# State space scan with head sums spread by one selector product, input stage merged with setup, narrow products by features, attention logits on both halves of the rows

## What is computed

```python
def mamba2_mixer(u, w_in, conv_w, conv_b, dt_bias, a_log, d_skip, norm_w, w_out):
    zxbcdt = u @ w_in                       # 1024 -> z 2048, xbc 4096, dt 32
    xbc = silu(causal_depthwise_conv(xbc, conv_w, conv_b))
    dt = softplus(dt_raw + dt_bias);  a = -exp(a_log)
    y = ssd_chunked_scan(xh * dt, dt * a, bm, cm)      # 32 heads in 8 groups
    ...
def stick_breaking_attention(u, w_q, k, v, w_o):       # 16 heads of 64
    z = einsum("bhqd,bhkd->bhqk", qi, kj)              # logits
    ...
```

## Time and profile before

| what | value |
|---|---|
| runs | 2638.74, 2640.85, 2643.32 us, median 2640.85 |
| profiled execution | 2641.31 us, span 2639.5 us |
| TensorE busy | 94% of the span |
| VectorE / ScalarE / GpSimd busy | 38% / 22% / 57% |
| mean granted TensorE clock | 0.964 of full |

### The profile page before, as it was taken

The page is one execution under the profiler, slowest core; times in us unless marked ns, Lnnn a source line. Parts: engine busy times, 40 slices in busy tenths (PEclk is TensorE's granted clock), DMA queues, the critical chain, the costliest instruction groups (busy, mean ns, idle before and its releaser), DMA issues.

```text
span 2639.5 us, 34935 instructions
## 1 busy us (share of the span) xinstructions
PE 2490.9 (94%) x14538; PEld 2019.2 (77%) x14538; DVE 1003.8 (38%) x1619; ACT 571.3 (22%) x1155; POOL 1494.0 (57%) x1396
## 2 busy tenths in 40 slices
PE   8998998999999999999999998998688998999998
PEld 6777886788888888558888887675477687888887
DVE  3443748155033400334512435775632332421023
ACT  1112322012011011760201101345443210110010
POOL 7554556568587486335867746471121664666663
PEclk9997999999999999999999998999798999999999
DMA  5222022223233233002332322130000232333321
GB/s 170 72 58 72 1 73 88 88 94 105 82 104 102 61 121 101 8 16 89 104 96 93 99 64 87 45 96 24 1 4 3 92 96 72 104 96 96 96 80 64
DMA packets 104290, 199.07 MB, mean 75 GB/s; under 512 B 9306, under 2 KB 12612, under 8 KB 104132
## 3 DMA queue, kind: packets, MB, share of 16 engines
q1 hardware_dynamic: 101476, 189.36, 23.0%
q10 hardware_dynamic: 2656, 7.47, 0.8%
HBM read 194.71 MB, written 2.10 MB: 75 GB/s over the span
## 4 chain that ended last, share of the span: by engine, by line
PE 84%; DVE 9%; ACT 3%; POOL 2%; issue 2%; SPq 0%; DMA 0%; DVEq 0%; POOLq 0%; ACTq 0%
PE psum L153 35%; PE psum L293 23%; PE psum L155 8%; PE psum L232 3%; PE psum L1253 1%; POOL weight_split_ring L412 1%; PE psum L968 1%; PE psum L1262 1%; PE psum L194 1%; DVE big L873 1%; PE psum L982 1%; PE psum L1281 1%; DVE big L1821 1%; DVE best L1820 1%; POOL weight_split_ring L409 0%
## 5 line engine op out<-in xcount | busy, mean ns | idle before, releaser
L412 POOL TENSOR_TENSOR weight_split_ring<-weight_ring,weight_split_ring 128x512 fp32r<-128x512 f32 (+2 forms) x732 | 953.6, 1323 | 30.6
L153 PE MATMUL psum<-x_split,weight_split_ring 128*128 128x512 f32 x4080 | 958.5, 394 | 1.9 <-POOL weight_split_ring L412 1.3
L153 PEld LDWEIGHTS psum<-x_split,weight_split_ring 128*128 128x128 f32 x4080 | 766.8, 189 | 171.9 <-issue 11.6
L409 POOL TENSOR_SCALAR weight_split_ring<-weight_ring 128x1024 fp32r<-128x1024 f32 (+2 forms) x366 | 395.2, 1080 | 735.2 <-PE psum L293 340.7
L293 PE MATMUL psum<-weight_split_ring,hidden_split 128*128 128x512 f32 x2448 | 576.6, 396 | 8.2 <-DVEq L2931 8.2
L293 PEld LDWEIGHTS psum<-weight_split_ring,hidden_split 128*128 128x128 f32 x2448 | 460.4, 188 | 120.0 <-DVEq L2931 8.6
L155 PE MATMUL psum<-weight_split_ring,x_split 128*128 128x512 f32 (+2 forms) x1056 | 240.5, 388 | 2.0 <-DVEq L2931 1.4
L155 PEld LDWEIGHTS psum<-weight_split_ring,x_split 128*128 128x128 f32 x1056 | 196.8, 207 | 44.5 <-issue 7.2
L708 DVE TENSOR_TENSOR big<-big 128x512 f32<-128x512 f32 x64 | 88.7, 1386 | 179.6 <-ACT big L693 179.6
L511 DVE SCALAR_TENSOR_TENSOR residual<-residual,psum 128x512 f32<-128x512 f32 x48 | 32.8, 683 | 262.2 <-PE psum L293 262.2
L693 ACT ACTIVATE big<-psum 128x512 f32<-128x512 f32 x64 | 38.3, 598 | 434.9 <-PE psum L153 378.9
(11 more groups left out here) (327 smaller groups left out, 2504.1 us busy)
## 6 DMA issues: line engine op xcount, KB each, us to landing
weight_ring<-in_mlp_w SPq DMA_DIRECT2D x128, 512.0 KB, 3.6
weight_ring<-in_w_in SPq DMA_DIRECT2D x92, 512.0 KB, 3.6
weight_ring<-in_w_ffn_in SPq DMA_DIRECT2D x40, 512.0 KB, 3.5
weight_ring<-in_w_out SPq DMA_DIRECT2D x24, 512.0 KB, 3.6
weight_ring<-in_w_ffn_out SPq DMA_DIRECT2D x22, 512.0 KB, 3.5
weight_ring<-in_sb_w_q SPq DMA_DIRECT2D x8, 512.0 KB, 3.6
weight_ring<-in_sb_w_k SPq DMA_DIRECT2D x8, 512.0 KB, 3.7
weight_ring<-in_sb_w_v SPq DMA_DIRECT2D x8, 512.0 KB, 3.6
```

The lines of the kernel that those rows point to most:

```text
L153: mm = pe.matmul(out, wp[:, k, m * P:(m + 1) * P], xp, start=first, stop=last)
L409: pool.tensor_scalar(part.high[:, 0:nk, 0:n], raw, 1.0, 0.0, ALU.mult, ALU.add).then_inc(self.high_made, 1)
L412: low = pool.tensor_tensor(part.low[:, k, 0:n], raw[:, k, :], part.high[:, k, 0:n].bitcast(F32), ALU.subtract)
```

## The change

1. `setup` is gone as a stage; `mamba_in` does its work and starts the wide products when x is split. The parameters are turned after two chunks.
2. The wide products come in the order: first part (tiles 0 to 3), `dt`, the other 28 tiles. `dt` is computed by features (one output tile of 32 rows, 24 products of 512 columns), turned by TensorE, and the chain of decays and sums runs under the products that follow. Turns of tiles come one at a time between rounds of products.
3. Decay sums: the running sums of all heads are also computed with heads on rows (`da_twice`, high and low half), and VectorE spreads them by head within group (`spread_sums`). In the scan one FP32R product with a group selector (`group_r`, 64 rows) replaces the four FP32 products of L968.
4. Attention logits: ScalarE's queue copies q and k (columns from 128 on) of each pair of heads, from the second pair on, to the other half of the rows; blocks 1 to 3 read the copy, block 0 the original.
5. `second_front`: the 72 narrow index columns are computed by features and turned by TensorE after two rounds of `ga`; VectorE's rotations wait for that copy.

```diff
-            kit.tiles += n // P if feature else NT
+            kit.tiles += -(-n // P) if feature else NT
...
-                            mm = pe.matmul(out, wp[:, k, m * P:(m + 1) * P], xp, start=first, stop=last)
+                            mm = pe.matmul(out, wp[:, k, m * P:m * P + rows], xp, start=first, stop=last)
...
+    g0 = Gemm(kit, w_in, KD, D_INNER, WIDE, True, banks=BK)
+    gd = Gemm(kit, w_in, KD, D_INNER + XBC, SSM_HEADS, True, banks=BK)
+    g1 = Gemm(kit, w_in, KD, D_INNER + WIDE, XBC - WIDE, True, banks=BK)
...
+        def turn_dt():
+            gd.wait_free(pe, 0)
+            pe.wait_ge(s_xh, PARAMETERS)
+            for c in range(NT):
+                mm = pe.transpose(kit.psum[:, 7, c * SSM_HEADS:(c + 1) * SSM_HEADS], m.dt_rows[:, c * P:(c + 1) * P],
+                                  m.ident[0:SSM_HEADS, 0:SSM_HEADS])
+            mm.then_inc(s_xt, 1)
+
+        def decay_sums():
+            pe.wait_ge(s_dt, DA)
+            pe.wait_ge(m.constants_cut, CONSTANT_STEPS)
+            for c in range(NT):
+                pe.matmul(kit.psum[:, 7, c * 32:c * 32 + 32], m.upper[:, :], m.da_twice[:, c, 0:SSM_HEADS], start=True, stop=True)
+                mm = pe.matmul(kit.psum[:, 7, P + c * 32:P + c * 32 + 32], m.ones[:, :], m.da_twice[:, c, 0:SSM_HEADS], start=True, stop=True)
+                mm = pe.matmul(kit.psum[0:2 * SSM_HEADS, 6, c * P:(c + 1) * P], m.da_twice[:, c, :], m.upper[:, :],
+                               start=True, stop=True)
+            mm.then_inc(s_xt, 1)
...
+        for n in range(2 * NT):
+            turn_x(n)
+        pe.wait_ge(s_xl, 2 * NT)
+        go_on(first, 8)
+        turn_parameters()
+        go_on(first, 8)
+        go_on(small, ROUNDS // NT)
+        for j in range(len(g1.parts)):
+            at = [9, 11, 13, 15] if j == 0 else [4, 7, 10, 13]
+            for r in range(ROUNDS):
+                if j == 0 and r == 2:
+                    turn_dt()
+                if j == 0 and r == 6:
+                    decay_sums()
+                if r in at and 4 * j + at.index(r) < TURNED:
+                    turn(4 * j + at.index(r))
+                go_on(wide, 1)
...
+        def spread_sums(half):
+            x = m.sums_r[:, 2 * P * half:2 * P * (half + 1)].bitcast(F32).rearrange("p (c l) -> p c l", l=P)
+            for r in range(HPG):
+                dve.tensor_scalar(m.sums_by_head[half][:, :, r, :], x, m.head_of_group[:, r:r + 1], None, ALU.mult)
...
+        for n in range(NT):
+            silu(n)
+        time_steps()
+        for n0 in range(NT, XBC_TILES, NT):
+            for n in range(n0 - NT, min(n0, TURNED)):
+                turned(n)
+            for n in range(n0, n0 + NT):
+                silu(n)
...
-            for r in range(HPG):
-                h = g * HPG + r
-                mm = pe.matmul(bank[:, r * P:(r + 1) * P], m.da[:, c, h:h + 1].broadcast_to([P, P]),
-                               m.upper[:, :], start=False, stop=True, skip_group_check=True)
-            mm.then_inc(s_cb, 1)
+            sums = m.sums_by_head[c // 2][:, c % 2].rearrange("p r l -> p (r l)")
+            pe.matmul(bank, m.group_r[:, g:g + 1].broadcast_to([2 * SSM_HEADS, P]), sums,
+                      start=False, stop=True, skip_group_check=True).then_inc(s_cb, 1)
...
+                    if n == 0:
+                        pe.wait_ge(s_sw[(h // 2) % 2], 32 * ((h // 2 + 1) // 2))
                 for b in blocks:
-                    mm = pe.matmul(bank(h, b), m.kF[rows(h), h // 2, b * P:(b + 1) * P], m.qF[rows(h), h // 2, b * P:],
-                                   start=(b != 3), stop=True, skip_group_check=True)
+                    if h >= 2 and b >= 1:
+                        k, q = other_k(h, b), other_q(h, b)
+                    else:
+                        k, q = m.kF[rows(h), h // 2, b * P:(b + 1) * P], m.qF[rows(h), h // 2, b * P:]
+                    mm = pe.matmul(bank(h, b), k, q, start=(b != 3), stop=True, skip_group_check=True)
...
+        def copy_halves(p):
+            if p >= 3:
+                act.wait_ge(s_z, NS * (2 * p - 2))
+            for g in range(2):
+                act.dma_start(m.swap[rows(g + 1), p % 2], m.qkF[rows(g), :, p, P:]).then_inc(s_sw[p % 2], 16)
...
+            if h % 2 == 0 and 2 <= h <= SB_HEADS - 6:
+                copy_halves(h // 2 + 2)
...
-    gi = Gemm(kit, w_in, KD, RW_COLS + 3 * ATT, IDXW, False)
+    gi = Gemm(kit, w_in, KD, RW_COLS + 3 * ATT, ATT, False)
+    gj = Gemm(kit, w_in, KD, RW_COLS + 4 * ATT, IDXW - ATT, True)
...
         gi.token_halves(pe, m.x_tile, before)
-        go_on(qkv, 8)
-
-        gi.wait_free(pe, gi.count - 1)
+        for _ in gj.stream(pe, m.x_tile):
+            pass
+        go_on(qkv, 2)
+        turn_narrow()
+        go_on(qkv, 6)
...
+        dve.wait_ge(s_tf, 1)
         for t in range(NT):
-            gi.wait_free(dve, NT + t)
```

More of the change, by code:

```diff
@@ new lines, in mamba_in, with tile, gemm, x_block @@
+    RAW, ABS, DA, TO_END, SPLIT_SUMS = 1, 2, 3, 4, 5
+    SUMS_READ, HIGH_SUMS, WEIGHT = 4, 5, 6
+    PARAMETERS, TURNED_DT, SUMS = 2 * NT + 1, 2 * NT + 2, 2 * NT + 3
+    LANDED = 16 * (len(ROWS) + 4)
+    nrow = sum(n for _, n in ROWS)
+    def tile(n):
+        return m.xring[:, n % 8, :] if n < X_TILES else m.bcF[:, n - X_TILES, :]
+    def gemm(n):
+        return (g0, n) if n < NT else (g1, n - NT)
+    def x_block(n):
+        t, j = n // 2, n % 2
+        return t, slice(4 * j, 4 * j + 4), slice(t * P, (t + 1) * P)
@@ L1199, in sb_attend @@
     s_z = kit.sem("sb_logits_ready")
+    s_sw = [kit.sem(f"sb_other_half_landed{n}") for n in range(2)]
     s_soft = kit.sem("sb_last_abs_then_exp_then_ln_ready")
@@ L1493, in go_on, with turn_narrow @@
                 next(stream)
+        def turn_narrow():
+            gj.wait_free(pe, 0)
+            for t in range(NT):
+                mm = pe.transpose(kit.psum[:, 5, t * NARROW:(t + 1) * NARROW], m.kidx[0:NARROW, block(t)],
+                                  m.ident[0:NARROW, 0:NARROW])
+            mm.then_inc(s_tr, 1)
         def turn_index(t):
@@ L2785, in __init__ @@
         self.bcF = self.part(b, 0, 2 * SSM_GROUPS, SEQ)
+        self.dt_rows = self.part(b, 14 * SEQ, SEQ)[0:SSM_HEADS, :]
+        pairs = 2 * SSM_HEADS
+        self.sums_r = self.hid.high[0:pairs, 15, :]
+        self.sums_by_head = [early[0:pairs], self.hid.low[0:pairs, 6:8, :].rearrange("p a b -> p (a b)")
+                             .rearrange("p (c r l) -> p c r l", c=2, r=HPG)]
         self.past_r = self.hid.low[:, 8, 0:P]
```

341 lines of the change are left out of this document (184 added, 157 removed).

## The result

The changed kernel takes **2618.41 us** (median of 4 runs, 2614.17 to 2621.19) where the kernel before took 2640.73 beside it: a ratio of 0.992, 95% interval 0.9908 to 0.9933. It is faster by 22 us, 0.8%; 56 were forecast, and 2618 lies above the range. The profiled execution took 2618.46 with a span of 2616.6, 22.9 less than the span before.

The account below looks back on a forecast made before the run. TensorE, busy nearly the whole span, was taken as the bound. Input stage -29.0, scan -14.1, logits -7 and second front -6 sum to -56.1, from 2641.3 to 2585 us; range 2564 to 2604.

Parts of the forecast that it names:

- Start and turning x and B: Input stage: earlier wide products -4.5 us, turns placed singly among products -13.6, less half clock between parts -4.
- dt and what is added: Input stage: dt by features -12.4 us; added transposes, decay sums and waits on TensorE +7.6 (ends 3.4 and 12).
- the last paragraph of the prediction: Signs to check; one sign of error was a clock falling at the new dt wait and costing over a microsecond.
- The wait of 1.0 ahead of the decay sums: Input stage: dt to its decays takes perhaps 6.5 us against four rounds = 5.5, so TensorE waits 1.0.
- The tail: End of the input stage: 11.4 us becomes 9.3, VectorE's last convolutions ending late: -2.1 us, 9 us idle before the scan.
- The scan: Scan stage: one FP32R selector product replaces four FP32 ones, 0.66 us a step less on TensorE; -14.1 us (ends -8 and -19).
- its first products are shorter: -2: Start of the scan: still at half clock after 9 us idle, but with shorter first products: -2 us.
- the selector product is no faster: Scan, part of the rival on halves not running side by side (chance 0.06): no product gain either, about 2604 us.
- Split logits: Attention: blocks 0 and 1 run together on different row halves, 0.5 us a head, 14 heads: -7 us (ends -12, +2).
- The other estimate, 4.5: Attention logits: if FP32 passes count as two products, 0.32 us a head, 4.5 in all, whole sum 2587.6.
- The late copies: Attention rival: q and k copies land late and TensorE waits; at 35 us landing +42, 2683 us; chance 0.03.
- Second front: Narrow index products: TensorE saves 11.2 us, rotations start earlier, two us taken for GpSimd's splits: -6 us (ends -11.2, +3).

Follow-up runs that it names:

- kernels with fillers: Changed kernel plus 46 unread products, 36 in the idle ahead of the scan, 10 in its first decay wait: 2597.80 us; with the selector on 128 rows too: 2589.93 us.
- the 128-row kernel: Changed kernel plus 46 unread products ahead of the scan and in its first decay wait, selector product padded with zero rows to 128: 2589.93 us, ratio 0.9804.
- the 36 fillers: Changed kernel plus 36 unread FP32R products in the 9.08 us in which TensorE idles ahead of the scan: 2616.59 us, ratio 0.9923.

## Why the prediction was wrong

**Start and turning x and B: right.** The wide products start at 13.67 (forecast 13.4), a turn costs 0.35 (65.24 to 65.59; forecast 0.40), none waits, and no stretch between the parts is at half clock.

**dt and what is added: right in the wait, wrong in its price.** The wait at the turns of dt is 2.84 (forecast 3.2), but in the profiled execution the granted clock was 0.50 there, from 48.0 to 54.8, which costs half of 6.8 us. The term left that out, though the last paragraph of the prediction named it. The clock doesn't fall each time: in the run without split logits the same 2.84 us of wait (48.49) had a granted 1.0 behind it, and its scan began 3.0 earlier. The wait of 1.0 ahead of the decay sums did not come, but their twelve products took 3.6 (57.41 to 61.00), not 2.7. The tail came as forecast: 9.08 idle ahead of the scan.

**The scan: the step that failed.** "One FP32r product of 512 columns (0.23 ...) replaces four FP32 ones (0.89): TensorE saves 0.66 a step." On 64 rows it costs 0.42, lengthens the product before it by 0.1 and those behind it by 0.1, while the earlier trace rows is on 128: the step saves 0.28, and the scan loses 7.5 us to it. And "the scan begins at half clock, in the new kernel too ... its first products are shorter: -2" took a return of the clock within five microseconds for granted because it had come. With the steps that hold a 64-row product it came 47 us into the scan, 20.2 us against a scan at full clock: -14.1 + 7.5 + 20.2 = 13.6, measured 13.9. That this adds up so well is partly luck, since both losses are read from kernels with fillers. Without fillers it is 24.4 for the 64 rows and 3.6 left over: on 128 rows the scan is 10.5 us shorter than before, not 14.1, for it ran at half clock for 10.8 us at its start where the kernel before did for 5.2. The steps themselves, 2.0, 3.1 and 2.2, are what the 128-row kernel shows at full clock: 2.01, 3.0 and 2.3. No rival had this; "the selector product is no faster" priced it at nothing gained, 2604 in all, and could not become a loss.

**Split logits: mechanism and TensorE's saving right, a wait left out.** The term was 0.5 a head, read from two products of equal length on the two halves. TensorE's logits became 0.43 and 0.54 shorter in the two heads of a pair, 0.97 together: 6.8 us over seven pairs, as forecast. But a pair gained only 0.79. Its busy time fell from 14.39 to 13.42 and its idle rose from 0.10 to 0.28, the 0.29 behind ScalarE (L1425) in the line at 1084.26: 5.5 us over seven pairs. The stage borders give 4.6. The other estimate, 4.5, took the passes for products of their own: the Trainium skill, "TensorE: Matmul & The Clock Gate", The mechanism, says that matmuls keep the order of the program. That 4.5 is close to what was measured is luck: it had block 0 beside the second pass of block 1 alone, and the rows above show it beside both. The late copies did not happen.

**Second front: the neighbour that was named, at more than its price.** TensorE's saving was there; VectorE's rotations beside GpSimd withheld it, most operations at 1.3 to 1.54 us instead of 0.45 (27 us from the first to the last, where 22 were before), and TensorE waited 1.01, 4.30 and 1.02 at the turns, with half clock from 1628.3 to 1631.7. I took two us for this; it was five. The Trainium skill, "SBUF — State Buffer", Who interferes with whom, has such instructions exclude each other whole. The key's 32-column operations agree in the run that rotates early, 0.18 us alone and up to 1.28 beside a split: what is paid goes mostly by the count of instructions, not by their size.

## What to carry to other kernels

A product that replaces others must be priced from a row with the same number of rows in its neighbours: one on 64 rows in a stream on 128 started 0.41 us behind the product before it and held up the next by 0.42, and padding it with zero rows to 128 was worth 24 us of the scan here, 7.5 of them by shorter steps at full clock and the rest by the clock. Where a stage starts at half clock, ask what brings the clock back, and whether the change removes it; steps with less work can be longer ones, and a few unread products in one short wait can be the cheapest repair. Beside a GpSimd that splits weights, make VectorE's instructions few and wide.

## What the runs showed that I had not expected

- At 1.2 GHz the profile shows TensorE busy 17.00 of 17.00 us (with the 36 fillers, 245 to 262), and the clock stays down; with the steps full at 2.4 GHz it stays up. The same 64-row steps did both, depending only on whether the wait behind the first two (2.3 us with fillers ahead of the scan) was filled. What exactly of a step counts for the clock (its rows, or the gaps of 0.2 us that they make) is not settled by these runs.
- More work made the scan shorter: 16 products more in chunk one ended it at 329.2 instead of 341.24 (one run).
- An earlier start was partly eaten: 5.1 us at the scan's start were 3.1 at the gate, since the half clock ended at the same time (272.9 and 273.2).
